# Splitting the first blocks ahead of TensorE's turn, and spacing out the tasks of a turn, in a fused two-block transformer kernel

## Chip, cores and metric

One core of a Trainium2 chip. The metric is the device time of one execution in microseconds; for the kernel before it is the median of three runs.

## What is computed

Two blocks of a network on 256 tokens of width 2048, all in fp32. The first block modulates its normed input with vectors made from a condition, and the change lies where that is done:

```python
mod_l = jnp.split(silu_c @ w_mod[l] + b_mod[l], 6, axis=-1)
mod_c = jnp.split(silu_cc @ w_mod[l] + b_mod[l], 6, axis=-1)
hl = modulate(rms_norm(xl, norm1_g[l]), mod_l[0], mod_l[1])   # h * (1 + scale) + shift
hc = modulate(rms_norm(xc, norm1_g[l]), mod_c[0], mod_c[1])
zl = hl @ w_in[l] + b_in[l]
zkv = hc @ w_in[l, :, K_OFF:G_OFF] + b_in[l, K_OFF:G_OFF]
```

Here `xl` is x and `xc` the context, 256 tokens too. Mixer, attention, feed-forward and a second block with 16 meta tokens follow. None of their code is changed.

## The kernel before

Weights come as blocks of 128 x 1024 fp32 (512 KB). A block lands in a `raw` buffer (L430). ScalarE copies it to a rounded hi half (`first_part`, L960), VectorE subtracts to get the lo half (`second_part`, L1542), and TensorE multiplies hi and lo with the activations, which are split in the same way: three products for one fp32 product. There are five hi and five lo buffers (`NSPLIT`), so ScalarE's split of unit u waits until TensorE is through with unit u-5.

`unit_plan` writes the order of all blocks down. The first 68 (`NSTART`) are the stage of the change. I call their places turns 0 to 67, and number block and turn alike. 64 of them are `w_mod`, in eight bands of eight: bands 0, 4, 1, 5, 2, 6, 3, 7 (`MOD0`), where bands 0 to 3 give the shift of a quarter of the columns, 4 to 7 its scale. Places 2 and 5 of each band (`WHOLE`, named "mod0") aren't split: TensorE takes them as fp32 (L601), straight from `raw`. The other six (named "mods") are units (L613). Four first halves of `w_in` stand at turns 48, 53, 58 and 63; they are units too, with 48 matmuls each (L512, L514, L517). Bands 0, 4, 1, 5, 2, 6 fill turns 0 to 47, bands 3 and 7 the rest.

Nine `raw` buffers serve this stage, block n in buffer n mod 9. From block 68 on it is n mod 4. SP issues the loads in order of the plan; each waits until the block that had the buffer before is free: after VectorE's lo half for a unit, after TensorE's matmuls for a whole block. In between SP loads `vec`, `cst`, x (after block 1) and ctx (after block 5).

Each engine runs the same turns in its own program. Work beside the blocks is in tasks (`Ticks`): a task is a generator, and a tick, at the end of each turn that isn't `w_in`, runs every active task to its next `yield`, in the order in which they were spawned. Engines wait for each other by semaphores. The tasks of this stage:
- `norms`: ScalarE squares two columns of x per tick in turns 0 to 7 (L981), GpSimd adds them up (L2281, L2284, two `sqr` buffers), TensorE makes the mean in turn 8 (L550), ScalarE the root (L990), VectorE the reciprocal (L1622), then the scaled input in turns 9 to 12 (L1628). For ctx the same: squares in turns 13 to 20, mean and root in 21, scaling in 22 to 25.
- `mod0_out`: when a band is done ScalarE copies its row out of PSUM (`mrow`, L1020), in the tick of the band's last turn. TensorE turns it in eight small matmuls two turns later (L578), and VectorE adds the bias (L1640, L1641).
- `modulate`: when bands g and g+4 are there, VectorE writes the modulated columns of four k into `tmp` (L1663, seven tiles), x's and ctx's, ScalarE copies them to `AH` and `CH` (L1034), VectorE writes `AL` and `CL` (L1668). g = 0 starts in turn 26, g = 1 in 34, g = 2 in 51, g = 3 after turn 67.

After turn 67 each engine starts the first splits of the next section (`first_parts(FIRST - 1)`: blocks 68 and 70 on ScalarE), runs all tasks to their end (`finish`), and goes on with the second halves of the four `w_in` units.

```python
for i in range(NSTART):              # scalar
    name, nb, q = plan[i]
    if name != "mod0":
        first_part(i)
    if name == "w_in":
        continue
    if q == 7:
        spawn(mod0_out(MOD0.index(nb), nb))
    tick()
first_parts(FIRST - 1)
finish(*ticks.active)
```

Of the kernel before, what the change touches and what calls it, by code (L numbers as in the profile page):

```python
# [7 lines left out]
F32 = mybir.dt.float32  # L8
F32R = mybir.dt.float32r
ALU = mybir.AluOpType  # L10
# [4 lines left out]
T = 256  # L15
# [5 lines left out]
AHEAD = 3  # L21
# [6 lines left out]
NSTART = 64 + NLEAD  # L28
# [75 lines left out]
def unit_plan():  # L104


    plan = []

    def full(name, m, kh=2):
        for h in range(kh):  # L110
            plan.append((name, m, h))

    def lead(name, m, h0=0):
        for h in range(2):
            for j in range(4):
                plan.append((name, m + j, h0 + h))

    mod = [("mod", nb, q) for nb in range(8, 24) for q in range(8)]
    mod0 = [("mod0" if q in WHOLE else "mods", nb, q) for nb in MOD0 for q in range(8)]
    plan += mod0[:NEARLY]  # L120
    share = (64 - NEARLY) // NLEAD
    for j in range(NLEAD):
        plan.append(("w_in", 40 + j, 0))
        plan += mod0[NEARLY + share * j:NEARLY + share * (j + 1)]
    for j in range(NLEAD):
        plan.append(("w_in", 40 + j, 1))
    for m in list(range(40 + NLEAD, 56)) + list(range(32, 40)) + list(range(24, 32)):
        full("w_in", m)
    for m in range(8):
        full("w_in", m)  # L130
        full("w_in", 8 + m)
    for m in range(16, 24):
        full("w_in", m)
    for g0, name in ((72, "w_sgu"), (88, "w_na"), (56, "w_conv")):
        for m in range(16):
            full("w_in", g0 + m)
            full(name, m, 1)
    for m in range(16):
        full("w_o", m)
    for c in range(4):  # L140
        if c == 0:
            lead("w_ff1", 0)
        for m in range(4 if c == 0 else 0, 16):
            full("w_ff1", 16 * c + m)
        lead("w_ff2", 0, 2 * c)
        for m in range(4, 16):
            plan.append(("w_ff2", m, 2 * c))
            plan.append(("w_ff2", m, 2 * c + 1))

    out = []  # L150
    for i, u in enumerate(plan):
        out.append(u)
        for _ in range(1 + i % 2 if NSTART <= i < 96 else 1 if i >= 176 and i % 5 < 2 + (i % 10 == 9) else 0):
            if mod:
                out.append(mod.pop(0))
    assert not mod and out.index(("mod", 19, 7)) < out.index(("w_conv", 14, 0))
    plan = out
    for h in range(8):
        for m in (16 + 2 * h, 17 + 2 * h, 2 * h, 2 * h + 1, 32 + 2 * h, 33 + 2 * h, 48 + 2 * h, 49 + 2 * h):
            full("w_ain", m)  # L160
    lead("w_aout", 0)
    for m in range(4, 16):
        full("w_aout", m)
    lead("w_pin", 0)
    for m in range(4, 32):
        full("w_pin", m)
    for g in range(4):
        plan += [("w_grp", g, 0), ("w_grp", g, 1)]
    lead("w_pout", 0)
    for m in range(4, 16):  # L170
        full("w_pout", m)
    return plan


def split_times(plan):


    act, dve, later = {FIRST - 1: []}, {FIRST - 1: []}, []
    place, use, done = NSTART, NSTART, set()
    n = sum(name != "mod" for name, _, _ in plan[NSTART:])  # L180

    def ahead(j, limit):
        nonlocal place
        while place < len(plan) and place <= limit:
            if plan[place][0] != "mod":
                act[j].append(place)
            later.append(place)
            place += 1

    ahead(FIRST - 1, use + AHEAD)  # L190
    for j in range(FIRST, FIRST + n):
        act[j], dve[j] = [], []
        while plan[use][0] == "mod":
            use += 1
        near = sum(plan[i][0] == "mod" for i in range(use, min(use + AHEAD + 3, len(plan))))
        dve[j] += later
        later.clear()
        ahead(j, use + AHEAD + min(near, 2))
        done.update(dve[j])
        while use not in done:  # L200
            dve[j].append(later[0])
            done.add(later.pop(0))
        use += 1
    return act, dve


def build(nc, ar, out_d):
    ctx = ExitStack()
    with ctx:
# [26 lines left out]
        tmp = [sb(f"tmp{i}", [128, L]) for i in range(7)]  # L236
# [13 lines left out]
        CH, CL = (sb(n, [128, 16, T], F32R, early, "right") for n in ("CH", "CL"))  # L250
# [120 lines left out]


        plan = unit_plan()
        act_at, dve_at = split_times(plan)
        unit_no, place_of, raw_free = {}, [], {}
        n_mod = n_m0p = 0
        raw_at, load_no, before, loads, last = [], [], [], [0] * (NRAW + NEXTRA), {}
# [571 lines left out]
        def _(e):  # L949
# [5 lines left out]
            def first_part(i):  # L955
                u = number_at[i]
                e.wait_ge(*landed(i))
                if u >= NSPLIT:
                    e.wait_ge(s_unit, u - NSPLIT + 1)
                e.activation(his[u % NSPLIT][:, :, :], raws[raw_at[i]][:, :].rearrange("p (k m) -> p k m", k=KU),  # L960
                             ACT.Copy).then_inc(s_hi, 1)
# [52 lines left out]
                    have.add(key)  # L1014

            def mod0_out(r, nb):
                e.wait_ge(s_unit, unit_no["mods", nb, 7] + 1)
                if r > 1:
                    e.wait_ge(s_m0t, r - 1)
                e.activation(mrow[r % 2][:, :], SS[r % 2][0:4, :], ACT.Copy).then_inc(s_m0e, 1)  # L1020
                yield
                yield
                have.add(nb)
                yield

            def modulate():
                n = 0
                for g in range(4):
                    while g not in have or 4 + g not in have or "ctx" not in have:
                        yield  # L1030
                    for k in range(4 * g, 4 * g + 4):
                        for hi in (A1H, CH):
                            e.wait_ge(s_mx, n + 1)
                            e.activation(hi[:, k, 0:T], tmp[n % 7][:, 0:T], ACT.Copy).then_inc(s_hx, 1)  # L1034
                            n += 1
                        yield

            spawn(norms())
            spawn(modulate())
            for i in range(NSTART):  # L1040
                name, nb, q = plan[i]
                if name != "mod0":
                    first_part(i)
                if name == "w_in":
                    continue
                if q == 7:
                    spawn(mod0_out(MOD0.index(nb), nb))
                tick()
# [473 lines left out]
        def _(e):  # L1522
# [121 lines left out]
                yield  # L1644

            def modulate():
                n = 0
                for g in range(4):
                    while g not in have or 4 + g not in have or "ctx" not in have:
                        yield  # L1650
                    e.wait_ge(s_m0v, 2 * g + 2)
                    for o, at in ((G1, 16), (G1C, 112)):
                        i = e.scalar_tensor_tensor(out=vt[:, o + 4 * g:o + 4 * g + 4],
                                                   in0=modv[:, at + 4 * g:at + 4 * g + 4], scalar=1.0,
                                                   in1=cols("n1g", 4, 4 * g), op0=ALU.add, op1=ALU.mult)
                    i.then_inc(*own.up())
                    done()
                    e.wait_ge(s_row, 2)
                    for k in range(4 * g, 4 * g + 4):
                        for v, (src, o, at) in enumerate(((XS, G1, 0), (ctxv, G1C, 96))):  # L1660
                            if n + v > 6:
                                e.wait_ge(s_lx, n + v - 6)
                            e.tensor_scalar(tmp[(n + v) % 7][:, 0:T], src[:, k, :], vt[:, o + k:o + k + 1],  # L1663
                                            modv[:, at + k:at + k + 1], ALU.mult, ALU.add).then_inc(s_mx, 1)
                        yield
                        for v, (hi, lo) in enumerate(((A1H, A1L), (CH, CL))):
                            e.wait_ge(s_hx, n + v + 1)
                            e.tensor_tensor(lo[:, k, 0:T], tmp[(n + v) % 7][:, 0:T], hi[:, k, 0:T].bitcast(F32),  # L1668
                                            ALU.subtract).then_inc(s_lx, 1)
                        n += 2  # L1670

            spawn(norms())
            spawn(modulate())
            for i in range(NSTART):
                name, nb, q = plan[i]
                if name != "mod0":
                    second_part(i)
                if name == "w_in":
                    continue
                if q == 7:  # L1680
                    spawn(mod0_out(nb))
                tick()
# [751 lines left out]
```

## Time and profile before

| | us |
|---|---|
| median of three runs | 2865.46 (2864.69 to 2871.01) |
| profiled execution, its own time | 2863.44 |
| its span, first to last instruction | 2861.5 |
| TensorE busy, by matmul records | 2719.5 |
| VectorE / ScalarE / GpSimd busy | 1918.5 / 1270.9 / 217.9 |
| mean granted TensorE clock | 0.973 of 2.4 GHz |

The span is the time that the rows divide; 1.9 us lie around it. The profiled execution is 2.0 us below the median. Busy shares are means over stages that differ; the stage of the change is the first 7%. A clock of 1.00 is 2.4 GHz, 0.50 is 1.2 GHz, and a value between is a stretch with both.

### The profile page before, as it was taken

The numbers are of one execution on the slowest core, as the hardware profiler recorded it, in microseconds if no ns is written. First come the engines' busy times: TensorE is split into PE (matmuls) and PEld (weight loads), VectorE is DVE, ScalarE is ACT, GpSimd is POOL, SyncE is SP. The second block draws the span as 40 slices with busy tenths as digits, with TensorE's granted clock in tenths as the row PEclk, the third lists the DMA queues.
The fourth block names the chain that finished last, engine by engine and source line by source line (L and its number), as shares of the span: only waits on it lengthen the run. The fifth ranks groups of instructions, "written<-read, shape, count | busy, mean of one in ns | idle before, by whom it ended". The sixth has DMA issues, their size and how long they took to land.

```text
span 2861.5 us, 51449 instructions
## 1 busy us (share of the span) xinstructions
PE 2719.5 (95%) x21378; PEld 2577.2 (90%) x21378; DVE 1918.5 (67%) x2951; ACT 1270.9 (44%) x1851; POOL 217.9 (8%) x212
## 2 busy tenths in 40 slices
PE   6789999899999899999999999999999998979996
PEld 2369987699999899999999999999999997979996
DVE  4645567788999787886564555577656665477564
ACT  4332244454434544644443444464444444444453
POOL 4000011200002300100000000021000000220011
PEclk8789999999999999999999999999999999989998
DMA  7546653264878687877555555554444443535553
GB/s 297 193 141 227 227 162 117 93 202 152 271 245 258 194 281 258 269 246 238 188 189 185 180 190 182 187 188 155 155 139 155 148 153 113 184 105 176 190 193 111
DMA packets 163991, 539.02 MB, mean 188 GB/s; under 512 B 31024, under 2 KB 35120, under 8 KB 163632
## 3 DMA queue, kind: packets, MB, share of 16 engines
q1 hardware_dynamic: 163760, 535.73, 56.7%
q8 instruction: 170, 2.79, 0.4%
q14 instruction: 61, 0.50, 0.1%
HBM read 533.57 MB, written 2.10 MB: 187 GB/s over the span
## 4 chain that ended last, share of the span: by engine, by line
PE 60%; DVE 5%; issue 1%; ACT 1%; POOL 0%; POOLq 0%; ACTq 0%; DVEq 0%
PE ps L512 19%; PE ps L517 19%; PE ps L514 19%; DVE lo L1542 1%; DVE row L2101 1%; PE ps L839 0%; DVE AL L2177 0%; PE ps L861 0%; PE ps L862 0%; DVE H L2185 0%; PE ps L550 0%; DVE ON L2109 0%; DVE Z L2265 0%; PE ps L937 0%; PE ps L933 0%
## 5 line engine op out<-in xcount | busy, mean ns | idle before, releaser
L960 ACT ACTIVATE hi<-raw 128x1024 fp32r<-128x1024 f32 x856 | 899.1, 1057 | 917.4 <-PE ps L517 456.1
L512 PE MATMUL ps<-AH,hi 128*128 128x256 f32 (+2 forms) x4480 | 1285.6, 287 | 18.8 <-DVE AL L2177 13.6
L517 PE MATMUL ps<-AH,lo 128*128 128x256 f32 (+2 forms) x4480 | 1272.8, 284 | 18.9 <-DVE lo L1542 18.9
L514 PE MATMUL ps<-AL,hi 128*128 128x256 f32 (+2 forms) x4480 | 1270.8, 284 | 0.0
L1542 DVE TENSOR_TENSOR lo<-raw,hi 128x1024 fp32r<-128x1024 f32 x856 | 1036.3, 1225 | 234.5 <-ACT hi L960 232.2
L512 PEld LDWEIGHTS ps<-AH,hi 128*128 128x128 f32 x4480 | 851.6, 190 | 52.2 <-issue 33.8
L517 PEld LDWEIGHTS ps<-AH,lo 128*128 128x128 f32 x4480 | 852.0, 190 | 22.8 <-DVE lo L1542 22.7
L514 PEld LDWEIGHTS ps<-AL,hi 128*128 128x128 f32 x4480 | 853.5, 191 | 0.9
L512 PE MATMUL ps<-YH,hi 128*128 128x256 f32 (+1 forms) x1536 | 433.8, 282 | 6.5 <-DVE YL L2112 6.5
L517 PE MATMUL ps<-YH,lo 128*128 128x256 f32 (+1 forms) x1536 | 432.9, 282 | 0.0
L514 PE MATMUL ps<-YL,hi 128*128 128x256 f32 (+1 forms) x1536 | 432.5, 282 | 0.0
L512 PEld LDWEIGHTS ps<-YH,hi 128*128 128x128 f32 x1536 | 290.8, 189 | 7.7 <-DVE YL L2112 7.6
L517 PEld LDWEIGHTS ps<-YH,lo 128*128 128x128 f32 x1536 | 291.6, 190 | 0.0
L514 PEld LDWEIGHTS ps<-YL,hi 128*128 128x128 f32 x1536 | 290.1, 189 | 0.0
L2284 POOL TENSOR_TENSOR ssum<-ssum,sqr 128x256 f32<-128x256 f32 (+1 forms) x142 | 146.3, 1031 | 270.8 <-ACT sqr L981 262.9
L2281 POOL COPY ssum<-sqr 128x272 f32<-128x272 f32 (+1 forms) x18 | 10.1, 566 | 1509.6 <-ACT sqr L981 1509.6
L1815 DVE SCALAR_TENSOR_TENSOR CV<-U,vec,CV 128x256 f32<-128x256 f32 x240 | 118.1, 492 | 4.3
L517 PE MATMUL ps<-BH,lo 128*128 128x256 f32 x384 | 107.3, 279 | 1.5 <-DVE lo L1542 1.5
L512 PE MATMUL ps<-BH,hi 128*128 128x256 f32 x384 | 107.3, 279 | 0.0
L514 PE MATMUL ps<-BL,hi 128*128 128x256 f32 x384 | 106.8, 278 | 0.0
L1961 DVE TENSOR_TENSOR tmp<-ps,rown 128x256 f32<-128x256 f32 x64 | 27.1, 424 | 111.8 <-PE ps L517 111.8
L1983 DVE SCALAR_TENSOR_TENSOR H<-ps,modv,H 128x256 f32<-128x256 f32 x48 | 23.3, 484 | 116.5 <-PE ps L517 116.5
(248 smaller groups left out, 2496.9 us busy)
## 6 DMA issues: line engine op xcount, KB each, us to landing
raw<-in_w_ff SPq DMA_DIRECT2D x256, 512.0 KB, 4.2
raw<-in_w_in SPq DMA_DIRECT2D x208, 512.0 KB, 4.4
raw<-in_w_mod SPq DMA_DIRECT2D x192, 512.0 KB, 4.5
raw<-in_w_ain SPq DMA_DIRECT2D x128, 512.0 KB, 3.6
raw<-in_w_pin SPq DMA_DIRECT2D x64, 512.0 KB, 3.5
raw<-in_w_o SPq DMA_DIRECT2D x32, 512.0 KB, 4.6
raw<-in_w_aout SPq DMA_DIRECT2D x32, 512.0 KB, 3.5
raw<-in_w_pout SPq DMA_DIRECT2D x32, 512.0 KB, 3.5
```

The lines of the kernel that those rows point to most:

```text
L512: e.matmul(b.ap[:, o], hi[:, k, :], xh, start=start and k + i == 0, stop=False, skip_group_check=many)
L514: e.matmul(b.ap[:, o], hi[:, k, :], xl, start=False, stop=False, skip_group_check=many)
L517: mm = e.matmul(b.ap[:, o], los[j % NSPLIT][:, k, :], xh, start=False, stop=stop and k == KU - 1, skip_group_check=many)
L960: e.activation(his[u % NSPLIT][:, :, :], raws[raw_at[i]][:, :].rearrange("p (k m) -> p k m", k=KU), ACT.Copy).then_inc(s_hi, 1)
L1542: e.tensor_tensor(los[u % NSPLIT][:, :, :], raws[raw_at[i]][:, :].rearrange("p (k m) -> p k m", k=KU), his[u % NSPLIT][:, :, :].bitcast(F3 ...
L1815: o = e.scalar_tensor_tensor(out=CV[:, m, :], in0=U[:, m, w:w + T], scalar=s, in1=CV[:, m, :], op0=ALU.mult, op1=ALU.add)
L1961: e.tensor_tensor(x[:, 0:T], b[:, 0:T], rown[:, 0:T], ALU.mult).then_inc(*own.up())
L1983: e.scalar_tensor_tensor(out=H[:, m, NM:L], in0=(tmp[m % 3] if c == 3 else b)[:, 0:T], scalar=g, in1=H[:, m, NM:L], op0=ALU.mult, op1=ALU. ...
L2101: e.reciprocal(r[:, 0:L], r[:, 0:L]).then_inc(*own.up())
L2281: e.tensor_copy(dst, src).then_inc(s_add, 1)
L2284: e.tensor_tensor(dst, dst, src, ALU.add).then_inc(s_add, 1)
```

## The change

ScalarE and VectorE no longer split a unit in its own turn. `early_times` lists for each turn the units that are split in it: all up to three units past the turn for ScalarE (`AHEAD` is 3), two for VectorE. ScalarE splits units 0 to 3 in turn 0, one more in each later turn that is a unit. The order of the splits stays. In the tasks, ScalarE's copy of a band's row is one tick later, its conversion of modulated columns too, and VectorE writes the lo columns of a k two ticks behind its `tmp` tiles instead of one.

```diff
--- before.py
+++ after.py
@@ -170,6 +170,18 @@
     for m in range(4, 16):
         full("w_pout", m)
     return plan
+
+
+def early_times(plan, lead):
+
+    places = [i for i in range(NSTART) if plan[i][0] != "mod0"]
+    at, n = [], 0
+    for i in range(NSTART):
+        seen = sum(p <= i for p in places)
+        upto = min(len(places), seen + lead)
+        at.append(places[n:upto])
+        n = max(n, upto)
+    return at
 
 
 def split_times(plan):
@@ -372,6 +384,7 @@
 
         plan = unit_plan()
         act_at, dve_at = split_times(plan)
+        act_early, dve_early = early_times(plan, AHEAD), early_times(plan, AHEAD - 1)
         unit_no, place_of, raw_free = {}, [], {}
         n_mod = n_m0p = 0
         raw_at, load_no, before, loads, last = [], [], [], [0] * (NRAW + NEXTRA), {}
@@ -1014,6 +1027,7 @@
                     have.add(key)
 
             def mod0_out(r, nb):
+                yield
                 e.wait_ge(s_unit, unit_no["mods", nb, 7] + 1)
                 if r > 1:
                     e.wait_ge(s_m0t, r - 1)
@@ -1028,19 +1042,21 @@
                 for g in range(4):
                     while g not in have or 4 + g not in have or "ctx" not in have:
                         yield
+                    yield
                     for k in range(4 * g, 4 * g + 4):
                         for hi in (A1H, CH):
                             e.wait_ge(s_mx, n + 1)
                             e.activation(hi[:, k, 0:T], tmp[n % 7][:, 0:T], ACT.Copy).then_inc(s_hx, 1)
                             n += 1
                         yield
+                    yield
 
             spawn(norms())
             spawn(modulate())
             for i in range(NSTART):
                 name, nb, q = plan[i]
-                if name != "mod0":
-                    first_part(i)
+                for p in act_early[i]:
+                    first_part(p)
                 if name == "w_in":
                     continue
                 if q == 7:
@@ -1644,7 +1660,16 @@
                 yield
 
             def modulate():
-                n = 0
+                n = n_low = 0
+
+                def low(k):
+                    nonlocal n_low
+                    for hi, lo in ((A1H, A1L), (CH, CL)):
+                        e.wait_ge(s_hx, n_low + 1)
+                        e.tensor_tensor(lo[:, k, 0:T], tmp[n_low % 7][:, 0:T], hi[:, k, 0:T].bitcast(F32),
+                                        ALU.subtract).then_inc(s_lx, 1)
+                        n_low += 1
+
                 for g in range(4):
                     while g not in have or 4 + g not in have or "ctx" not in have:
                         yield
@@ -1662,19 +1687,20 @@
                                 e.wait_ge(s_lx, n + v - 6)
                             e.tensor_scalar(tmp[(n + v) % 7][:, 0:T], src[:, k, :], vt[:, o + k:o + k + 1],
                                             modv[:, at + k:at + k + 1], ALU.mult, ALU.add).then_inc(s_mx, 1)
+                        n += 2
+                        if k > 4 * g + 1:
+                            low(k - 2)
                         yield
-                        for v, (hi, lo) in enumerate(((A1H, A1L), (CH, CL))):
-                            e.wait_ge(s_hx, n + v + 1)
-                            e.tensor_tensor(lo[:, k, 0:T], tmp[(n + v) % 7][:, 0:T], hi[:, k, 0:T].bitcast(F32),
-                                            ALU.subtract).then_inc(s_lx, 1)
-                        n += 2
+                    low(4 * g + 2)
+                    yield
+                    low(4 * g + 3)
 
             spawn(norms())
             spawn(modulate())
             for i in range(NSTART):
                 name, nb, q = plan[i]
-                if name != "mod0":
-                    second_part(i)
+                for p in dve_early[i]:
+                    second_part(p)
                 if name == "w_in":
                     continue
                 if q == 7:
```

## Rows read from the trace of the kernel before

**Rows 1.** Windows by stage: us; busy (x) of PE, PEld, DVE, ACT, POOL; PEclk; DMA share; GB/s
```profile
0.00:67.81 67.81, 43.29 (x109) 18.55 (x109) 31.88 (x55) 31.93 (x55) 30.06 (x36) 0.87 0.82 304
67.81:139.63 71.82, 51.04 (x131) 21.68 (x130) 42.54 (x80) 28.65 (x43) 0.00 (x0) 0.79 0.55 185
139.63:196.17 56.54, 50.20 (x272) 38.15 (x272) 24.75 (x38) 17.93 (x24) 0.00 (x0) 0.91 0.41 143
...
212.00:2861.50 2649.50, 2567.55 (x20826) 2491.62 (x20824) 1806.81 (x2751) 1186.40 (x1719) 187.86 (x176) 0.98 0.57 187
```

**Rows 2.** Waits in 67.81 to 139.63 us: total, times, longest
```profile
ACT AH L1034 <- DVE tmp L1663: 21.6, 8, 5.4
...
ACT mrow L1020 <- PE ps L613: 20.8, 4, 10.2
...
PE ps L613 <- ACT hi L960: 12.4, 8, 2.0
...
PE ps L613 <- DVE lo L1542: 6.6, 10, 1.3
```

**Rows 3.** Timeline at a change of band: start us, us, engine, line, operation [idle before]
```profile
98.66 0.59 ACT L1020 ACTIVATE mrow<-ps 4x512 f32<-4x512 f32 x1 [2.93 <-PE ps L613]
...
100.34 0.70 PE L613 MATMUL ps<-hi,CS 128*128 128x512 f32 x2 [1.71 <-ACT hi L960]
...
101.51 1.22 PE L613 MATMUL ps<-lo,CS 128*128 128x512 f32 x2 [0.47 <-DVE lo L1542]
```

**Rows 4.** Loads at L430: block 6 alone, all issues in 0 to 30 us, page part 6
```profile
L430 SPq DMA_DIRECT2D raw<-in_w_mod x1: 432/432/432, 11.2 to 11.2; - x1
...
DMA to landing us min/median/max: 15.4/15.4/15.4
...
DMA to landing us min/median/max: 5.3/10.5/17.8
...
raw<-in_w_mod SPq DMA_DIRECT2D x192, 512.0 KB, 4.5
```

**Rows 5.** GpSimd's adds of squares of x: timeline, and min/median/max ns
```profile
17.41 15.98 POOL L2284 TENSOR_TENSOR ssum<-ssum,sqr 128x256 f32<-128x256 f32 x14 [0.31 <-ACT sqr L981]
...
L2284 POOL TENSOR_TENSOR ssum<-ssum,sqr x15: 724/728/1537, 16.4 to 32.7; 128x256 f32<-128x256 f32 x15
```

**Rows 6.** Groups of VectorE in 0 to 210 us: busy us, mean ns, idle before
```profile
L1542 DVE TENSOR_TENSOR lo<-raw,hi 128x1024 fp32r<-128x1024 f32 x54 | 65.4, 1235 | 51.5 <-ACT hi L960 51.5
...
L1628 DVE TENSOR_TENSOR G<-G,row 128x256 f32<-128x256 f32 x16 | 5.7, 418 | 0.0
...
L1668 DVE TENSOR_TENSOR AL<-tmp,AH 128x256 fp32r<-128x256 f32 x16 | 6.7, 421 | 1.1 <-ACT AH L1034 1.1
...
L1622 DVE RECIPROCAL row<-row 128x256 f32<-128x256 f32 x2 | 3.5, 1754 | 5.5 <-ACT row L990 5.5
```

**Rows 7.** Timeline: a whole block (L601) at either clock, the mean over ctx
```profile
42.81 3.58 PE L601 MATMUL ps<-raw,vt 128*2 128x512 f32 x4
...
67.81 0.70 PE L550 MATMUL ps<-ssum,ones 128*128 128x256 f32 x2
...
134.07 1.88 PE L601 MATMUL ps<-raw,vt 128*2 128x512 f32 x4
```

**Rows 8.** Timeline of the last starting turns and the last modulation
```profile
194.09 0.33 SPq L430 DMA_DIRECT2D raw<-in_w_in  x1
...
196.17 0.59 ACT L1020 ACTIVATE mrow<-ps 4x512 f32<-4x512 f32 x1 [12.09 <-PE ps L613]
...
197.87 1.06 ACT L960 ACTIVATE hi<-raw 128x1024 fp32r<-128x1024 f32 x1 [0.17 <-DMA raw<-in_w_in]
...
198.50 0.41 DVE L1663 TENSOR_SCALAR tmp<-VTok,vt,modv 128x256 f32<-128x256 f32 x1
...
198.83 0.41 DVE L1663 TENSOR_SCALAR tmp<-G,vt,modv 128x256 f32<-128x256 f32 x1
...
204.77 1.22 DVE L1542 TENSOR_TENSOR lo<-raw,hi 128x1024 fp32r<-128x1024 f32 x1
```

## Prediction

> **What bounds the kernel now.** I read the windows first, cut where the order of work changes [rows 1]. From 212 us to the end TensorE is busy 2567.6 of 2649.5 us at a granted clock of 0.98. The change touches nothing there, so a microsecond won ahead of it should be a microsecond off the end. The 68 starting turns look different. In turns 22 to 47 (67.81 to 139.63 us) TensorE is busy 51.0 of 71.8 us at clock 0.79; in turns 48 to 67 (to 196.17 us) it is busy 50.2 of 56.5 us at 0.91. ScalarE, VectorE and the DMA engines are at 40, 59 and 55% in the first of the two: nobody is the bound, they wait in turn.
>
> The waits say for whom [rows 2]. ScalarE stands 20.8 us for TensorE's last matmul of a band and 21.6 us for VectorE's modulated tile; TensorE stands 12.4 us for a hi half and 6.6 us for a lo half. One change of band shows the circle [rows 3]: the copy of the band's row waits for TensorE and starts at 98.66, the next hi half can only come behind it, TensorE restarts at 100.34 after 1.71 us without work, then stops again for the lo half and runs it at half clock (1.22 us for two matmuls).
>
> **The change, part by part.** *The lead.* ScalarE splits to three units past its turn, VectorE to two. A hi buffer is reused after five units, so ScalarE at unit u needs TensorE through with u-2: when it stops for a band's last matmul, TensorE still has four split units before it. The waits for hi and lo halves [rows 2] should all but go. No instruction is added or removed; the splits keep their order, and so do the loads on SP.
>
> *The start, turns 0 to 21: a small loss.* Turn 1 of ScalarE now begins with the split of block 6, issued at 11.2 us and landed 15.4 us later, at 26.6 [rows 4]. Behind it in the queue stand the squares of x from the third on, which before had no load to wait for but x. GpSimd's adds follow: 14 adds took 15.98 us in one piece, 1.14 us each [rows 5]. New: 26.6 + 1.04 for the split + 16.0 = 43.7 us, where it was 33.4. TensorE's mean of turn 8 waits for that, then root and row copy reach 46 us. Now ScalarE is also tied to loads: its turn 15 splits block 19, whose buffer TensorE frees with the whole block of turn 10 (1.88 us at full clock, 3.58 at half [rows 7]), at about 51; plus 4.5 us landing [rows 4] is 55.5. Turn 17 needs block 22, freed at turn 13: 59.5. The last four pairs of ctx squares follow, 8 x 1.14 = 9.1 us, and the mean of turn 21 is at about 69.5, against 67.8 now [rows 7]: **+1.7**. Low end: three more splits bring ScalarE to turn 13 at 49, and GpSimd alone from there gives 49 + 16 x 1.14 = 67.2. High end: every add at the 1.54 us maximum [rows 5] adds 32 x 0.4 = 13 us less what was already slow; I keep 76.
>
> On that row a rule bears. An add takes 724 ns alone and up to 1537 ns [rows 5], the long ones beside a lo split. The Trainium skill (GPSIMD Engine Reference, Key points) says that GpSimd and VectorE share SBUF interfaces and contend when a VectorE instruction has two SBUF inputs, as the lo split has. By it more splits beside more adds would mean up to the 76 above; since the count of splits per add does not change, I stay with 1.14.
>
> *Turns 22 to 47: the gain.* With the waits gone the stretch costs what its busiest engine needs. VectorE [rows 6, 8]: 19 lo halves x 1.235 = 23.5; a reciprocal 1.75; 16 ctx scalings x 0.42 = 6.7; two groups of modulation, 32 instructions at 0.33 from start to start = 10.6; small ones about 1; mean and root ahead of it 1.2: 44.8 us. TensorE: 51.0 busy, less what half clock added. Clock 0.79 means 42% of 71.8 = 30 us at half, at most 15 too many: 36 us or a little more. Loads: 27 blocks in 46 us is 308 GB/s, just the 304 of the first window [rows 1]. So VectorE is the bound, TensorE close below it. Two engines that close disturb each other, and while TensorE is at half clock it is the slower one; I add 1.2 and take **46 us instead of 71.8**. Turn 48 starts at 69.5 + 46 = 115.5 instead of 139.6: **-24.1** with the start's loss in it. Ends: 41 (splits back to back, no disturbance) and 55 (TensorE's 36 at the clock of today, 46, plus half of VectorE's hand-overs).
>
> *Turns 48 to 67.* Four w_in units lie in between, TensorE is the bound. It idles 56.5 - 50.2 = 6.3 us, and clock 0.91 is 10.2 us at half, 5.1 too many [rows 1]. The lead removes the idle time but for 0.5 and leaves about one spell at half, 1.7: **-9.2**; I count -8.9 for gaps of issue. Ends -5 and -11.
>
> *The tail: a loss.* The added yield puts the last band's row copy behind the first splits of the next section on ScalarE. The second of them, block 70, is issued only when TensorE frees its buffer at turn 65 (194.09), and is split from 197.87 to 198.93; before, the copy went ahead of it at 196.17 [rows 8]. So the copy comes 2.76 us later, and the eight transposes, the last modulation and the lo half that TensorE waits for come behind it. The modulation itself is shorter: 198.50 to 204.77 now, 6.27 us; two tiles apart, it is 16 instructions x 0.33 = 5.3 [rows 8]. **+2.8 - 1.0 = +1.8**. Elsewhere the copy is moved behind splits too, but of blocks long landed.
>
> *Tasks spaced out.* ScalarE converts a block one turn after VectorE wrote it, VectorE takes the lo two turns after. Both already waited for less; the seven tmp tiles are enough for three blocks. In its own right nothing: it is what lets the 21.6 us of waits [rows 2] go, and without it the lead would be lost in turns 26 to 37.
>
> Sum: -24.1 - 8.9 + 1.8 = **-31.2 us**. The profiled execution took 2863.44, so 2832.2; the median of the runs is 2865.46, 2.0 above: **2834 us**.
>
> **The rivals.**
> A, *the norms cost more*: the ctx squares wait at each turn for a late load, mean of turn 21 at 76 or more. For it: both squares and rows are strictly behind the splits. Against: 4.5 us landings once the queue is not full. Gain 31 - 7 to 31 - 14: 2841 to 2848. Chance 0.14.
> B, *TensorE at 1.2 GHz*: it now idles from about 37 to 44 us and some 8 us ahead of turn 21, and the clock was 0.79 for a TensorE that is busy 71% [rows 1]. At half clock all through turns 22 to 47 it needs 36 x 2 = 72 us, so that gain is gone: 1.7 - 5 + 1.8 = -1.5, 2864. With half the stretch so it takes 54 us: 1.7 - 17.8 - 7 + 1.8 = -21.3, 2844. The Trainium skill (TensorE: Matmul & The Clock Gate, HAM oscillation) says that a TensorE that keeps waiting between bursts falls back to 1.2 GHz each time; by it VectorE's pace would keep the clock swinging. Against: 0.98 where TensorE is busy 97% [rows 1]. Chance 0.10 for 2842 to 2855.
> C, *better than I think*: VectorE at 41, turns 48 on at -11, no start loss: gain 38 to 42, 2824 to 2828. Chance 0.12.
> D, *slower*: the loads become the loop. ScalarE's unit at turn t+5 needs a load that TensorE released at t-4, so nine turns take at least landing + 1.04 + 1.24 + 1.88. Today nine turns take 71.8 / 26 x 9 = 24.9. It decides from a landing of about 20.7 us; the longest of the crowded start is 17.8 [rows 4]. At 22 us, 26 turns take 75.6, the same loop eats the gain of turns 48 to 67, and with start and tail 3.8 + 3.5 = 7 us are lost: 2873. Chance 0.03.
> E, *the change doesn't do what it says*: the hi buffers or the row copy still hold ScalarE to TensorE's turn, all stays within 5 us. Against: the count of five above. Chance 0.02.
>
> **How the numbers follow.** Forecast 0.59 (2828 to 2841), A 0.14, B 0.10, C 0.12, D 0.03, E 0.02. The range runs from C to the end of A: 2823 to 2848, leaving out most of B, D and E and the far end of C. 0.2%, or 5.7 us, is what a measurement of this kernel can tell. All of the forecast, A, B and C lie beyond it: faster 0.95, same 0.02, slower 0.03.
>
> **What would show it.** Right: the wait of the mrow copy stays but TensorE's waits for hi and lo in turns 22 to 47 fall from 19 to under 4 us; the x adds end near 44; mean of turn 21 near 69; turn 48 near 115; last row copy after the split of block 70, about 2.8 us behind its matmul; clock in turns 48 to 67 at 0.95 or more; the window from the first second-half unit on unchanged. Wrong: a mean of turn 21 beyond 76 (A), clock under 0.75 in turns 22 to 47 (B), or ScalarE waiting for loads at most turns (D).

## Result and profile after

The changed kernel takes 2837.04 us (median of four runs, 2836.03 to 2839.6), the kernel before 2865.89 beside it (2864.69 to 2871.01). The ratio is 0.9897, 95% interval 0.988 to 0.9914: 28.9 us or 1.0% faster. The forecast was 2834 within 2823 to 2848.

The page of the profile after, its span, busy times and clock in 40 slices:

```profile
span 2834.1 us, 51449 instructions
...
PE 2707.5 (96%) x21378; PEld 2579.3 (91%) x21378; DVE 1917.5 (68%) x2951; ACT 1271.6 (45%) x1851; POOL 222.6 (8%) x212
...
PEclk7999999999999999999999999999999999989998
```

Span and TensorE's busy time shrink by 27.4 and 12.0 us; the instructions are the same. Where the time went is in the windows, cut at the same events as [rows 1]: the mean over ctx, the first matmul of turn 48, the end of turn 67, TensorE's restart on the first second-half unit. Columns as there: us; busy (x) of PE, PEld, DVE, ACT, POOL; PEclk; DMA share; GB/s.

```profile
0.00:74.18 74.18, 43.78 (x109) 20.69 (x109) 32.83 (x57) 35.05 (x58) 35.27 (x36) 0.79 0.74 278
74.18:119.32 45.14, 39.71 (x131) 20.40 (x131) 41.86 (x80) 27.28 (x40) 0.00 (x0) 0.89 0.75 274
119.32:162.86 43.54, 43.54 (x273) 33.15 (x271) 22.07 (x36) 17.91 (x24) 0.00 (x0) 1.00 0.56 207
174.38:2834.10 2659.72, 2579.05 (x20858) 2503.82 (x20858) 1813.79 (x2758) 1187.06 (x1719) 187.34 (x176) 0.98 0.57 187
```

- Up to the mean over ctx (turn 21) the kernel is slower: 74.18 us instead of 67.81, **+6.4**.
- Turns 22 to 47 take 45.14 us instead of 71.82, **-26.7**. VectorE, busy 59% of this stretch before, is now busy 41.86 of 45.14 us, 93%.
- Turns 48 to 67 take 43.54 us instead of 56.54, **-13.0**: TensorE has no idle time there and its clock is 1.00 instead of 0.91.
- From there to the restart it is 11.5 us (162.86 to 174.38) instead of 9.9 (196.17 to 206.04): **+1.7**.

At the restart the kernel is 31.7 us ahead. From there to the end it takes 2659.7 us where the kernel before took 2655.5.

The waits in turns 22 to 47 (total, times, longest) answer to [rows 2]:

```profile
ACT AH L1049 <- DVE tmp L1688: 10.9, 4, 7.2
...
PE ps L626 <- DVE lo L1558: 5.4, 4, 2.5
...
ACT hi L973 <- DMA raw<-in_w_mod: 4.6, 5, 1.4
```

ScalarE's 20.8 us for TensorE's last matmul of a band and TensorE's 12.4 us for hi halves no longer appear among the waits of this stretch; ScalarE's wait for modulated columns is halved, 21.6 to 10.9 us. TensorE's wait for lo halves is nearly what it was (6.6 before), which fits a VectorE without spare time. New are 4.6 us in which ScalarE waits for loads.

### The profile page after: what moved, and what is told of

Same layout as the page of the kernel before. It is cut to its first block, busy times and chain, and to the rows that moved or that the text cites. A ratio compares the mean times of both kernels' runs of the same rounds, so it can differ in the third digit from the quotient of the medians.

```text
span 2834.1 us, 51449 instructions
## 1 busy us (share of the span) xinstructions
PE 2707.5 (96%) x21378; PEld 2579.3 (91%) x21378; DVE 1917.5 (68%) x2951; ACT 1271.6 (45%) x1851; POOL 222.6 (8%) x212
## 4 chain that ended last, share of the span: by engine, by line
PE 61%; DVE 5%; issue 1%; ACT 1%; POOL 0%; POOLq 0%; ACTq 0%; DVEq 0%
PE ps L525 19%; PE ps L530 19%; PE ps L527 19%; DVE lo L1558 1%; DVE row L2127 1%; PE ps L852 0%; DVE AL L2203 0%; PE ps L874 0%; PE ps L875 0%; DVE H L2211 0%; PE ps L563 0%; DVE ON L2135 0%; DVE Z L2291 0%; PE ps L947 0%; PE ps L946 0%
## 5 line engine op out<-in xcount | busy, mean ns | idle before, releaser
L525 PEld LDWEIGHTS ps<-AH,hi 128*128 128x128 f32 x4480 | 849.5, 190 | 45.6 <-issue 33.8
L530 PEld LDWEIGHTS ps<-AH,lo 128*128 128x128 f32 x4480 | 851.5, 190 | 19.3 <-DVE lo L1558 19.2
```

Of the source, the lines that this page charges most:

```text
L525: e.matmul(b.ap[:, o], hi[:, k, :], xh, start=start and k + i == 0, stop=False, skip_group_check=many)
L530: mm = e.matmul(b.ap[:, o], los[j % NSPLIT][:, k, :], xh, start=False, stop=stop and k == KU - 1, skip_group_check=many)
```

## The experiments

All of them change the first 68 turns and the tasks run out behind them, nothing else. This table has the events of each profile, in us from the start of the span, and the median of the runs; the first column is the mean over x in turn 8. Times of "before" beside the experiments were 2865.1 to 2866.7 (median of seven).

| kernel | mean x | mean ctx | turn 48 | restart | median |
|---|---|---|---|---|---|
| before | 35.8 | 67.8 | 139.6 | 206.0 | 2865.89 |
| before, second profile | 35.0 | 67.0 | 138.8 | 205.1 | 2864.11 (one run) |
| changed | 43.4 | 74.2 | 119.3 | 174.4 | 2837.04 |
| lead only | 43.0 | 74.3 | 119.9 | 173.4 | 2834.33 |
| spaced tasks only | 35.0 | 68.4 | 119.5 | 174.9 | 2835.07 |
| row copy first | 43.8 | 74.6 | 119.8 | 172.3 | 2832.03 |
| late lead | 34.0 | 68.0 | 113.6 | 169.6 | 2829.45 |
| late lead, row copy first | 34.4 | 68.4 | 113.9 | 166.3 | 2825.57 |
| lead from turn 22, row copy first | 35.3 | 68.8 | 117.4 | 169.8 | 2831.31 |
| row copy a tick later, alone | 34.3 | 67.9 | 126.6 | 184.3 | 2846.76 |
| spaced modulation alone | 34.8 | 66.8 | 128.5 | 187.2 | 2847.14 |
| scaling of x moved | 43.3 | 70.4 | 121.5 | 177.2 | 2840.73 (one run) |

### Which part gives the gain: e1_lead_only and e2_tasks_only

The change has two parts, so each was run alone. The lead alone is the kernel before with the two new lists:

```diff
-                if name != "mod0":
-                    first_part(i)
+                for p in act_early[i]:
+                    first_part(p)
...
-                if name != "mod0":
-                    second_part(i)
+                for p in dve_early[i]:
+                    second_part(p)
```

> The lead of three and two units, with the tasks of a turn as they were before. Theory L (the lead takes TensorE's waits for hi and lo halves away): turns 0 to 47 stay near what the changed kernel shows except where columns are modulated (turns 26 to 37), where ScalarE and VectorE wait for each other in the same turn; the row copy of the last band is not behind the split of block 70, so the tail is 2.7 us shorter and the modulation in it 1.0 longer. Median 2834 to 2845. Theory S (the spacing of the tasks brings the gain, the lead little): 2858 to 2868.

Measured: 2834.33 us (2832.45 to 2837.72), ratio 0.9894 (0.9877 to 0.991). Turns 22 to 47 take 45.6 us, as with both parts. From the last row copy to the restart it is 9.9 us (163.49 to 173.37), as before the change: the copy isn't behind a split, and the modulation isn't shortened. This is theory L's number.

The spaced tasks alone are the changed kernel with no lead:

```diff
-        act_early, dve_early = early_times(plan, AHEAD), early_times(plan, AHEAD - 1)
+        act_early, dve_early = early_times(plan, 0), early_times(plan, 0)
```

> The spaced tasks, with every unit split in its own turn as before. Theory L: no gain; the row copy now stands behind one more split at each band, TensorE waits longer there: 2862 to 2872. Theory S: 2838 to 2848.

Measured: 2835.07 us (2834.5 to 2838.59), ratio 0.9897 (0.9882 to 0.9911). This is below both theories' numbers, and theory L, which e1_lead_only had borne out, is 27 us off. **Each part alone gives the whole gain**, and together they give no more. Their ways differ. Without a lead turns 22 to 47 take 51.1 us (68.4 to 119.5), 5.5 more than with it, but the start isn't lost, 68.4 instead of 74.3. Both reach turn 48 within half a microsecond of each other. The waits of the spaced tasks alone in turns 22 to 47:

```profile
ACT mrow L1034 <- PE ps L626: 8.5, 3, 3.8
PE ps L626 <- DVE lo L1558: 8.3, 14, 1.2
ACT AH L1049 <- DVE tmp L1688: 8.1, 4, 3.8
...
PE ps L626 <- ACT hi L973: 1.5, 1, 1.5
```

TensorE still waits 1.5 us for hi halves and 8.3 for lo halves, in small pieces: that is what the lead removes on top. The big waits of [rows 2] are cut down without it. (Three of the four row copies fall in this window; the fourth comes just behind it and waits another 3.6 us, 12.1 in all where before had 20.8.)

### Which of the spaced tasks: e6_row_yield and e7_mod_spacing

The first is the kernel before with one yield, the second the changed kernel without lead and without that yield:

```diff
             def mod0_out(r, nb):
+                yield
                 e.wait_ge(s_unit, unit_no["mods", nb, 7] + 1)
```

> The kernel before with one yield more, ahead of ScalarE's copy of a band's row: the copy then stands behind the first split of the next band. Theory R (the circle at a change of band holds the engines, and one unit ahead is enough to open it): in turns 22 to 47 most of the 20.7 us that the spaced tasks gave are there, median 2836 to 2845. Theory M (the circle is in the modulation, whose hand-overs fall in one turn): at most 2.2 us at each of eight changes of band, less the 2.7 of the tail, median 2850 to 2860.

Measured: 2846.76 us (2845.17 to 2847.01), ratio 0.993 (0.9915 to 0.9945): between the two theories.

> The spaced modulation alone: no lead, the row copy in the tick of the band's last turn as before. Theory R: the changes of band still cost what they did, median 2850 to 2862. Theory M: the 21.6 us that ScalarE waited for modulated columns go, turn 48 at 120 to 126 us, median 2836 to 2845.

Measured: 2847.14 us (2844.21 to 2851.86), ratio 0.9934 (0.9918 to 0.9951). This too lies between them, so neither theory holds: there are two circles, and each edit opens one. In turns 22 to 47 the one yield leaves, in its kernel's waits (67.87 to 127.5 us, 0.9 us into turn 48, so that all four row copies are in),

```profile
ACT AH L1035 <- DVE tmp L1664: 17.1, 7, 6.1
...
ACT mrow L1021 <- PE ps L613: 10.9, 4, 3.8
```

and the spaced modulation leaves, in its own,

```profile
ACT mrow L1033 <- PE ps L626: 20.6, 4, 10.2
...
ACT AH L1048 <- DVE tmp L1687: 11.7, 4, 5.2
```

The yield cuts ScalarE's wait for TensorE's last matmul of a band from 20.8 to 10.9 us and hardly touches the wait for modulated columns (21.6 to 17.1). The spaced modulation does the reverse: 20.6 and 11.7. They are worth 19.2 and 18.8 us beside their own runs of before, 38.0 together, and 30.0 when both are in (2865.12 - 2835.07): so 8 us are counted in both. Which wait they share wasn't measured.

### The loss at the start: e4_late_lead and e8_scale_later

The start costs 6.4 us, where 1.7 were forecast. First the order on ScalarE. These rows of the changed kernel's timeline show it (start us, us, engine, line, operation, idle before):

```profile
18.39 1.06 ACT L973 ACTIVATE hi<-raw 128x1024 fp32r<-128x1024 f32 x1 [0.22 <-DMA raw<-in_w_mod]
...
19.36 0.71 ACT L994 ACTIVATE sqr<-H 128x256 f32<-128x256 f32 x2
...
25.85 1.06 ACT L973 ACTIVATE hi<-raw 128x1024 fp32r<-128x1024 f32 x1 [5.79 <-DMA raw<-in_w_mod]
...
26.81 0.71 ACT L994 ACTIVATE sqr<-H 128x256 f32<-128x256 f32 x2
...
27.29 15.96 POOL L2310 TENSOR_TENSOR ssum<-ssum,sqr 128x256 f32<-128x256 f32 x14 [5.44 <-ACT sqr L994]
...
43.39 1.19 PE L563 MATMUL ps<-ssum,ones 128*128 128x256 f32 x2 [7.97 <-POOL ssum L2310]
```

The two squares of turn 0 run at 19.36, behind the split of block 4. Then the third square waits until 26.81, for it stands behind the split of block 6, whose load lands at 25.8. GpSimd's adds start at 27.29 instead of 17.41 and end at 43.25 instead of 33.39 [rows 5]. TensorE waits 7.97 us for its mean. The experiment holds the lead back:

```diff
-        upto = min(len(places), seen + lead)
+        upto = min(len(places), seen + (lead if i >= 9 else 0))
```

> The changed kernel with the lead only from turn 9 on, so that no square of x stands behind a load still on its way. If the order on ScalarE makes the loss of the start: the adds of x end near 33.4 us as in the kernel before instead of 43.3, the mean of turn 21 comes at 64 to 69 us instead of 74.2, the restart 5 to 10 us earlier: median 2827 to 2832. Rival (the loss of the start is made in turns 13 to 20, by loads freed late and GpSimd held up by VectorE): the adds of x end at 33.4 but the mean of turn 21 stays at 72 or later, median 2834 to 2838.

Measured: 2829.45 us (2828.36 to 2829.75), ratio 0.9874 (0.9859 to 0.9889). The adds of x run as before the change, in the late lead's timeline:

```profile
15.82 15.99 POOL L2310 TENSOR_TENSOR ssum<-ssum,sqr 128x256 f32<-128x256 f32 x14 [0.30 <-ACT sqr L994]
```

They end at 31.8 us. The mean over ctx is at 68.0 and the median 2829.45, both within the ranges expected; the restart is 4.7 us earlier, a little short of the 5 to 10. Turns 22 to 47 take 45.6 us, 45.1 in the changed kernel.

From the mean over x to the mean over ctx, though, the changed kernel takes 30.8 us where the forecast had 25.5. Its timeline shows one thing that no row of before has:

```profile
53.77 1.21 DVE L1558 TENSOR_TENSOR lo<-raw,hi 128x1024 fp32r<-128x1024 f32 x1
...
54.91 1.42 DVE L1644 TENSOR_TENSOR VTok<-H,row 128x256 f32<-128x256 f32 x4
...
56.25 3.49 DVE L1558 TENSOR_TENSOR lo<-raw,hi 128x1024 fp32r<-128x1024 f32 x3
...
54.25 7.80 POOL L2310 TENSOR_TENSOR ssum<-ssum,sqr 128x256 f32<-128x256 f32 x3 [4.17 <-ACT sqr L994]
...
55.18 1.06 ACT L973 ACTIVATE hi<-raw 128x1024 fp32r<-128x1024 f32 x1 [0.70 <-DMA raw<-in_w_mod]
...
60.35 0.42 ACT L994 ACTIVATE sqr<-G 128x256 f32<-128x256 f32 x1 [4.11 <-POOL ssum L2310]
...
74.18 0.67 PE L563 MATMUL ps<-ssum,ones 128*128 128x256 f32 x2 [1.30 <-POOL ssum L2310]
```

and the add that starts at 54.25, alone (min/median/max ns):

```profile
L2310 POOL TENSOR_TENSOR ssum<-ssum,sqr x1: 6067/6067/6067, 54.3 to 54.3; 128x256 f32<-128x256 f32 x1
```

**It takes 6067 ns.** The longest of before is 1537 [rows 5]. VectorE runs from 53.77 to 59.74 without a gap, a split, four scalings of x and three more splits, which the lead had made ready for it; the add ends at 60.3 and the next square can only then start, 4.11 us late. To test this, the scalings were moved behind the sums:

```diff
+                    if key == "x":
+                        for _ in range(4):
+                            yield
+                        continue
...
+                        for kk, s, d in (("x", H[:, :, NM:L], XS), ("ctx", ctxv, ctxv)):
+                            i = e.tensor_tensor(d[:, k, :], s[:, k, :], rows[ROW[kk] % 2][:, 0:T], ALU.mult)
```

> The changed kernel with VectorE's sixteen scalings of x moved out of turns 9 to 12 into turns 22 to 25, beside those of ctx. In the changed kernel one add of GpSimd took 6067 ns from 54.3 us on, while VectorE ran scalings and splits without a gap. If VectorE's unbroken run is what holds it up, the longest add is under 2 us here and the mean of turn 21 comes 3 to 5 us earlier than 74.2, near 70; turn 48 does not gain as much, since VectorE has 5.7 us more to do after it. Rival (the loads hold ScalarE, the long add costs nothing): the mean of turn 21 stays at 73 to 75.

Its adds in all, and its mean over ctx:

```profile
L2316 POOL TENSOR_TENSOR ssum<-ssum,sqr x30: 721/726/1544, 21.0 to 69.5; 128x256 f32<-128x256 f32 x30
```

```profile
70.41 0.67 PE L563 MATMUL ps<-ssum,ones 128*128 128x256 f32 x2 [1.42 <-POOL ssum L2316]
```

The long add is gone and the mean comes at 70.41 us, 3.8 earlier; the mean over x is where it was (43.3). So breaking up VectorE's run gives back 3.8 of the 4.7 us by which the forecast was off. Late loads did not do it: the split of block 19 at 55.18 waits 0.70 us for its load. The same run bears on what bounds turns 22 to 47: they take 51.1 us instead of 45.1, with 5.7 us of scalings moved into them, and VectorE is busy 46.8 of the 51.1 us, 92%. Work added to VectorE there is paid in full.

### The tail: e3_row_first

The end of the changed kernel's start stage, in its timeline:

```profile
160.81 0.33 SPq L443 DMA_DIRECT2D raw<-in_w_in  x1
...
164.57 1.06 ACT L973 ACTIVATE hi<-raw 128x1024 fp32r<-128x1024 f32 x1 [10.83 <-DMA raw<-in_w_in]
...
165.53 0.57 ACT L1034 ACTIVATE mrow<-ps 4x512 f32<-4x512 f32 x1
...
167.84 0.41 DVE L1688 TENSOR_SCALAR tmp<-VTok,vt,modv 128x256 f32<-128x256 f32 x1
...
173.11 1.22 DVE L1558 TENSOR_TENSOR lo<-raw,hi 128x1024 fp32r<-128x1024 f32 x1
...
174.38 0.58 PE L530 MATMUL ps<-AH,lo 128*128 128x256 f32 x1 [6.68 <-DVE lo L1558]
```

TensorE is through with turn 67 at 162.86. The row copy starts at 165.53, behind the split of block 70, which waits for its load, issued at 160.81. The next lines are the modulation, the lo half and the restart. The experiment lets the copy go first:

```diff
+            tick()
             first_parts(FIRST - 1)
             finish(*ticks.active)
```

> The changed kernel with one more tick on ScalarE ahead of the splits of blocks 68 and 70, so that the last band's row copy goes first. By the prediction's tail term the copy starts with TensorE's last matmul instead of 2.7 us behind it, and TensorE's restart on the first second-half unit (174.4 us in the changed kernel) comes at 171.7: median 2834.4. Rival: the restart then waits for something else (ScalarE's splits come behind the conversions of the modulation), under 1 us: 2836 to 2838.

Measured: 2832.03 us (2831.2 to 2832.46), ratio 0.9883 (0.9868 to 0.9898). Its timeline has the copy ahead of the two splits:

```profile
163.41 0.59 ACT L1034 ACTIVATE mrow<-ps 4x512 f32<-4x512 f32 x1 [12.10 <-PE ps L626]
...
163.90 2.20 ACT L973 ACTIVATE hi<-raw 128x1024 fp32r<-128x1024 f32 x2
```

From turn 48 to the restart it takes 52.45 us instead of 55.06: 2.6 us, as forecast. The median is 2.4 us below the 2834.4 expected. In the two profiles 1.5 us of the gain lie behind the restart, where single executions scatter (below), but all four runs of this kernel are below all four of the changed one, by 3.6 us at least. Where the rest of the gain comes from stays open.

### Putting the two together: e5_both, e9_lead_22

> Late lead and row copy first together. The restart of the late lead was 169.6 us, and the row copy first was worth 2.1 us at the restart of the changed kernel: if the two add up the restart is at 167.5 and the median 2827.3. Rival: the earlier tail only brings the wait for the first splits forward, median 2829 to 2830 as with the late lead alone.

Measured: 2825.57 us (2824.67 to 2828.26), ratio 0.9859 (0.9844 to 0.9873). This is the fastest version, 11.5 us below the changed kernel. Its tail:

```profile
155.35 0.33 SPq L443 DMA_DIRECT2D raw<-in_w_in  x1
...
157.43 0.59 ACT L1034 ACTIVATE mrow<-ps 4x512 f32<-4x512 f32 x1 [12.09 <-PE ps L626]
...
159.14 1.06 ACT L973 ACTIVATE hi<-raw 128x1024 fp32r<-128x1024 f32 x1 [0.17 <-DMA raw<-in_w_in]
...
166.30 0.58 PE L530 MATMUL ps<-AH,lo 128*128 128x256 f32 x1 [6.69 <-DVE lo L1559]
```

The copy waits for TensorE alone, and the split of block 70 comes behind it. The restart is at 166.30, 1.2 us earlier than adding the two would give, and the median 1.7 us lower. In the late lead alone TensorE had no work for 3.5 us ahead of the eight transposes and ran them at half clock, in 1.83 us (granted clock 0.50); here it idled 0.77 us and they took 1.02 at full clock. That is 0.8 of the 1.2 us.

> The row copy first, and the lead only from turn 22 on, when the sums for both norms are done. If the lead is worth nothing in turns 9 to 21 (the mean of turn 21 was at 67.8 to 68.4 us with late lead, with none and before), this is level with the late lead and row copy first (2825.6): 2824 to 2828. If the lead in turns 9 to 21 fed turns 22 to 30, turn 48 comes 2 us or more later and the median is 2828 to 2831.

Measured: 2831.31 us (2827.27 to 2832.62), ratio 0.9873 (0.9857 to 0.989). The mean over ctx is where it is with the lead from turn 9 on, 68.8 us, but turn 48 comes 3.5 us later. The median is 0.3 us above the range expected for that case. So the lead in turns 9 to 21 doesn't bring the mean forward, it has splits done by then that VectorE needn't do afterwards: 18 lo halves were begun before the mean over ctx, here 16, and two are about 2.4 of the 3.5 us.

### The rest of the kernel: b2_before_again

> The kernel before once more, for a second profile. From TensorE's restart on the first second-half unit to the end the kernels don't differ, yet it took 2655.5 us in the profile of before and 2658.0 to 2661.7 in those of the nine others. If that is scatter of single executions, this profile lies between 2656 and 2661. If an earlier start makes the rest slower, it lies at 2655 to 2656 again.

Its rest takes 2657.1 us, in the range of scatter. It is the second shortest of twelve, though, and the first profile of before is the shortest; the ten others have 2658.0 to 2661.7. So a part of the 4.3 us that the profiles lose behind the restart is scatter, and whether some 2 us of it belong to an earlier restart stays open. No edit tried here orders them: the lead alone has 2658.4, both parts 2659.7.

## Why the prediction was right, and where not

- **The start, +1.7 forecast, +6.4 measured.** The first half of the step held: the adds of x were put at 43.7 and end at 43.25. The term that failed is the second half, from there to the mean over ctx at "about 69.5". It priced every add at 1.14 us, with 1.54 as the most a row showed. One add took 6.07, 4.9 more than its price, and with the scalings moved away it and 3.8 us of the loss are gone. The load chain in the same step held: the split of block 19 starts at 55.18, forecast 55.5. The 76 us kept as the high end held the 74.2, but not by its reason, which was every add at 1.54.
- **Turns 22 to 47, 46 us forecast, 45.1 measured.** Right, and for the reason given: VectorE is the bound (93% busy, and 5.7 us of work added to it cost 5.9). The terms met less well than the sum: 43.6 us of work and 1.2 of waiting were counted for VectorE, and it was busy 41.9 and idle 3.3. The 16 ctx scalings were put at 6.7 us by their mean duration, where the same row of [rows 6] has 5.7 busy, since neighbours overlap; and 21 lo halves fell in the stretch, not 19. Two of the signs failed. TensorE's waits were to fall under 4 us; they are 5.4, all for lo halves. And "the wait of the mrow copy stays": in the changed kernel none of the eight row copies waits for TensorE. The clock was 0.89.
- **Turns 48 to 67, -8.9 forecast, -13.0 measured.** The mechanism held, idle time gone and clock up. The size was off: I left one spell at half clock and some idle time, and there was neither. This is beyond the end of -11 that I gave.
- **The tail, +1.8 forecast, +1.7 measured**, with its cause shown by the row copy first.
- **"Tasks spaced out ... in its own right nothing"**: this step is wrong, and so is "without it the lead would be lost in turns 26 to 37". Alone the spaced tasks give 30.0 us, and the lead alone loses nothing in those turns. I took the waits of [rows 2] for one circle that only the lead could open. There are two, at the change of band and in the modulation, as the two halves of the spaced tasks show, and each part of the change opens both. How they do it is read from the order of the work: a lead of three units has work ready, and a waiting task moved a turn back has a unit of work ahead of its wait.
- **The sum.** Forecast -31.2, at the restart -31.7: the start cost 4.7 more than forecast and turns 48 to 67 gave 4.1 more. The total is so close because two errors of size met, which is luck. The medians differ by 28.9: 4.3 us are lost behind the restart in the profiles, and the profile of before is 2.5 us under its median, that of after 1.0.
- **The rivals.** A: the mean over ctx at 74.2 is near its 76, and 4.7 of its 7 to 14 us were lost, but not by its mechanism, late loads at each turn: 3.8 of the 4.7 were the one long add. C: turns 48 to 67 reached its end and passed it, the rest did not come. B: half clock in turns 22 to 47 fell from 42 to 22% of the time. D: ScalarE waits 4.6 us for loads there, but TensorE doesn't wait for a hi half.

## What to carry to other kernels

When engines take turns in waiting for each other, count how many units of work stand ahead of each wait in its own queue; one already took about half of each wait away here, and the two kinds of spacing together gave as much as a lead of three units. A lead costs where the work put ahead waits for something of its own, a load on its way or a buffer freed late: hold it back until the crowded first loads have landed, and put a short copy that others wait for ahead of it. And once the waits were gone, a sum over the busiest engine's work came close: 44.8 us were counted, 45.1 measured. An engine's work packed without gaps can hold up another engine, though, as with the add of 6.07 us, and a mean duration from the kernel before doesn't price that.

## What the runs showed of the hardware

An add on GpSimd of 128x256 fp32 takes 0.72 us alone and up to 1.54 us beside a lo split on VectorE (in the late lead, where a short VectorE instruction and a split follow each other, one took 1.76). It took 6.07 us where VectorE ran eight instructions with two SBUF inputs end to end, seven of them begun after the add; in the lead alone and the row copy first, with the same run beside them, the longest were 6.31 and 5.99. VectorE's own instructions were not slowed there (1.42 us for four scalings). Where an add had begun first (49.36 us in the changed kernel), the four scalings from 49.56 on took 1.81 us.

The Trainium skill (SBUF — State Buffer, SBUF: two separate sides) says of a GpSimd instruction and a VectorE one with two SBUF inputs that whichever starts first holds the shared pair of ports for its whole instruction while the other is blocked. The 1.54 us and the 1.81 us fit that. The 6.07 us go beyond it: the add waited not for one instruction but lasted as long as the whole run (54.25 to 60.3, the run ends at 59.74). That GpSimd doesn't get its turn between VectorE's instructions is the reading of three such adds in three kernels; nothing shorter or longer than this run of eight was tried.
